# A decoder trunk in fp32: C of the state-space layer moved from the kernel's opening into the first up-projection, in two halves

## What is computed

```python
cs = silu(c)
for i in range(2):
    mod = cs @ ada_w[i] + ada_b[i]
    sh1, sc1, g1, sh2, sc2, g2 = split(mod, 6)
    h = rms_norm(x, norm1_g[i]) * (1 + sc1) + sh1
    mix = dilated_attention(h) if i == 0 else s5_mixer(h)
    x = x + g1 * mix
    h = rms_norm(x, norm2_g[i]) * (1 + sc2) + sh2
    x = x + g2 * conv_ffn(h)          # up-projection 2048 -> 2 * 5632, conv, silu(gate) * up, down
return rms_norm(x, final_norm_g)

# s5_mixer: lb = exp(a * step); coef = (lb - 1) / a; bb = coef * b
# x_t = lb * x_(t-1) + bb u_t ;  y_t = Re(c x_t) + d u_t
```

## Time and profile before

| | us |
|---|---|
| median of 3 runs | 2718.42 (2717.45 to 2720.98) |
| the profiled execution | 2721.41 |
| its span, first to last instruction | 2719.6 |
| PE busy | 2653.0 |
| VectorE busy | 2276.5 |
| ACT busy | 1293.0 |
| GpSimd busy | 512.4 |

### The profile page before, as it was taken

The page is one execution under the profiler, slowest core; times in us unless marked ns, Lnnn a source line. Parts: engine busy times, 40 slices in busy tenths (PEclk is TensorE's granted clock), DMA queues, the critical chain, the costliest instruction groups (busy, mean ns, idle before and its releaser), DMA issues.

```text
span 2719.6 us, 50038 instructions
## 1 busy us (share of the span) xinstructions
PE 2653.0 (98%) x18416; PEld 2377.3 (87%) x18416; DVE 2276.5 (84%) x3379; ACT 1293.0 (48%) x1869; POOL 512.4 (19%) x468
## 2 busy tenths in 40 slices
PE   5999999999999999999999999999999999999998
PEld 1998888888898888888888999999888888888887
DVE  6978988888889998899998988998898975677754
ACT  2444444444434655435555344444365553455543
POOL 4142201101133111000101321244411110011122
PEclk8999999999999999999999999999999999999999
DMA  9979989888876987678888968879777765655563
GB/s 377 394 254 346 339 313 344 315 318 321 317 236 219 317 285 256 203 246 307 282 284 269 375 230 250 240 250 328 256 248 250 263 182 188 200 187 190 183 191 117
DMA packets 242267, 725.47 MB, mean 267 GB/s; under 512 B 51106, under 2 KB 60066, under 8 KB 241186
## 3 DMA queue, kind: packets, MB, share of 16 engines
q1 hardware_dynamic: 185184, 666.46, 70.8%
q10 hardware_dynamic: 56900, 56.54, 6.5%
HBM read 701.66 MB, written 25.44 MB: 267 GB/s over the span
## 4 chain that ended last, share of the span: by engine, by line
PE 85%; DVE 2%; POOL 2%; issue 1%; DMA 1%; ACT 0%; ACTq 0%; POOLq 0%; DVEq 0%
PE proj L1929 28%; PE proj L1956 15%; PE proj L1936 14%; PE proj L1959 8%; PE proj L1979 5%; PE proj L1981 4%; PE proj L1980 4%; PE proj L1974 2%; PE proj L1961 1%; PE proj L1977 1%; PE ps L2102 1%; PE ps L2192 1%; DVE w_lo L1202 0%; POOL work L1785 0%; POOL work L1787 0%
## 5 line engine op out<-in xcount | busy, mean ns | idle before, releaser
L606 ACT ACTIVATE w_hi<-raw 128x1024 fp32r<-128x1024 f32 (+1 forms) x896 | 929.7, 1043 | 1118.0 <-PE proj L1936 350.8
L1202 DVE TENSOR_TENSOR w_lo<-raw,w_hi 128x1024 fp32r<-128x1024 f32 (+1 forms) x896 | 1109.9, 1244 | 352.1 <-ACT w_hi L606 341.6
L1929 PE MATMUL proj<-h_hl,w_hi 128*128 128x512 f32 x2656 | 633.7, 391 | 1.7 <-DVE x L1532 1.7
L1929 PEld LDWEIGHTS proj<-h_hl,w_hi 128*128 128x128 f32 x2656 | 488.5, 188 | 97.0 <-DVE x L1532 2.1
L1092 DVE SCALAR_TENSOR_TENSOR ada<-ada,held 128x1024 f32<-128x1024 f32 x304 | 392.5, 1291 | 0.0
L1956 PE MATMUL proj<-h_hl,w_hi 128*128 128x512 f32 x1500 | 381.0, 394 | 0.9 <-DVE work L1388 0.9
L1936 PEld LDWEIGHTS proj<-h_hl,w_lo 128*128 128x128 f32 x2656 | 340.5, 191 | 12.9
L1936 PE MATMUL proj<-h_hl,w_lo 128*128 128x256 f32 x2656 | 344.5, 283 | 0.0
L1835 POOL TENSOR_TENSOR a_hl<-work,a_hl 128x256 fp32r<-128x256 f32 (+1 forms) x88 | 119.6, 1359 | 1135.0 <-ACT a_hl L896 1135.0
L1956 PEld LDWEIGHTS proj<-h_hl,w_hi 128*128 128x128 f32 x1500 | 272.9, 189 | 51.6 <-DVE work L1388 1.2
L1979 PE MATMUL proj<-a_hl,w_hi 128*128 128x256 f32 x864 | 245.7, 284 | 0.8 <-DVE a_hl L1423 0.6
(11 more groups left out here) (287 smaller groups left out, 3369.6 us busy)
## 6 DMA issues: line engine op xcount, KB each, us to landing
raw<-in_w_up SPq DMA_DIRECT2D x352, 512.0 KB, 5.0
ada<-in_ada_t SPq DMA_DIRECT2D x304, 512.0 KB, 5.6
raw<-in_w_in SPq DMA_DIRECT2D x224, 512.0 KB, 6.4
raw<-in_w_down SPq DMA_DIRECT2D x128, 448.0 KB, 4.2
raw<-in_w_down SPq DMA_DIRECT2D x64, 512.0 KB, 3.7
ada<-in_ada_w SPq DMA_DIRECT2D x48, 512.0 KB, 9.1
raw<-in_w_out SPq DMA_DIRECT2D x32, 512.0 KB, 5.0
raw<-in_ssm_w_in SPq DMA_DIRECT2D x32, 512.0 KB, 4.9
```

What stands on the lines that cost most here:

```text
L606: nc.scalar.activation(w_hi[:, j % LAG, 0:nk * P], raw[:, j % s.ring, 0:nk * P], ACT.Copy).then_inc(hi_ready, 1)
L1202: V.tensor_tensor(w_lo[:, j % LAG, 0:nk * P], raw[:, j % s.ring, 0:nk * P], w_hi[:, j % LAG, 0:nk * P].bitcast(F32), ALU.subtract).then_in ...
L1929: mm(proj[b % 2][:, :], w_hi[:, j % LAG, (k - k0) * P:(k - k0 + 1) * P], hl[:, k].rearrange("p c t -> p (c t)"), start=(k == 0), stop=False)
```

## The change

C's load leaves the list of constants (nine instead of ten), and its buffer in the opening goes. In the first pass of the first up-projection ACT loads one half of C into `work` at step 6, at step 12 stores it once GpSimd has multiplied it and then loads the other half into the same place, and stores that at step 18. GpSimd multiplies a half in six products of 128 x 512, at its steps 0 and 14. The store in `qkv1` and the waits on it before `qkv` go; the first `load_c` waits for both stores.

GpSimd builds the table of powers first; its first part waits for the sum of squares, whose place the table takes. SP no longer waits for GpSimd's products before it loads into slot 6 of the ring.

The first eight columns of the first scale, gain * (1 + bias + sum), are made in the sums: VectorE spreads gain and gain * (1 + bias) over lanes (`gain_diag`, `bias_diag`) beforehand, PE adds the second to the running sum with four products at piece 26 of 32, and VectorE multiplies and reduces (`take_scale`) where it had multiplied, reduced, added the bias and applied the gain.

```diff
@@ build: places
-        c_raw, o = cut(a_flat, 24 * T, TILES, 2, SC)
-        lam, o = cut(a_flat, o, KT, CHUNK, 4, 2)
+        lam, o = cut(a_flat, 32 * T, KT, CHUNK, 4, 2)
-        t16a, _ = cut(raw_flat, (RAW - 1) * MODW, TILES, SC)
-        t16b, _ = cut(raw_flat, (RAW - 2) * MODW, TILES, SC)
+        c_half, o = cut(work, 0, TILES // 2, 2, SC)
+        t16a, o = cut(work, o, TILES // 2, SC)
+        t16b, o = cut(work, o, TILES // 2, SC)
+        bias_diag, o = cut(a_flat, 5 * T, MODB, 32)
+        gain_diag, _ = cut(a_flat, o, MODB, 32)
@@ SP, weights
                         sp.wait_ge(ada_summed, 2 * KT)
-                        wait(sp, prep_done, j // 6)
@@ ACT
-            act.dma_start(c_raw, a["ssm_c"]).then_inc(consts_in, 16)
...
-            act.wait_ge(consts_in, 16 * 10)
+            act.wait_ge(consts_in, 16 * 9)
...
-            def store_cw(i):
-                act.wait_ge(prep_done, 1)
-                act.dma_start(cw_d.rearrange("n p f -> p n f"), c_raw.rearrange("p (n q) a b -> p n (q a b)", q=4)
-                              ).then_inc(cw_out, 16)
...
-            late = {1: [store_lam], 8: [load_rel], 14: [store_cw], 22: [spread_lam(0)], 26: [spread_lam(1)]}
+            late = {1: [store_lam], 8: [load_rel], 22: [spread_lam(0)], 26: [spread_lam(1)]}
...
-            act.wait_ge(cw_out, 16)
...
+                            if n == 0:
+                                act.wait_ge(cw_out, 32)
...
+            def load_c_half(h):
+                def f():
+                    act.wait_ge(norm_lo, 2 * KT)
+                    wait(act, cw_out, 16 * h)
+                    act.dma_start(c_half, a["ssm_c"][:, h * TILES // 2:(h + 1) * TILES // 2]).then_inc(consts_in, 16)
+                return f
+
+            def store_c_half(h):
+                def f():
+                    act.wait_ge(prep_done, h + 1)
+                    act.dma_start(cw_d[h * KT // 2:(h + 1) * KT // 2].rearrange("n p f -> p n f"),
+                                  c_half.rearrange("p (n q) a b -> p n (q a b)", q=4)).then_inc(cw_out, 16)
+                return f
...
-                carry = {}
+                carry = {} if layer else {6: [load_c_half(0)], 12: [store_c_half(0), load_c_half(1)], 18: [store_c_half(1)]}
@@ VectorE
+            def take_scale():
+
+                dve.wait_ge(ada_summed, 2 * KT)
+                V.tensor_tensor(diag, first_ps[1], gain_diag, ALU.mult).then_inc(mod_ready, 1)
+                dve.wait_ge(mod_ready, 2)
+                V.tensor_reduce(hscale[:, 0:MODB], diag, AX.X, ALU.add).then_inc(scale_made, 1)
+                dve.wait_ge(scale_made, 2)
...
-            V.tensor_copy(hscale[:], gains[:, 0, :]).then_inc(coef_made, 1)
-            take_first(0)
+            V.tensor_scalar(hscale[:, 0:MODB], mod_b[:, 0, KT:KT + MODB], 1.0, None, ALU.add).then_inc(scale_made, 1)
+            dve.wait_ge(scale_made, 1)
+            spread = lambda v: v.unsqueeze(2).broadcast_to([P, MODB, 32])
+            V.tensor_tensor(gain_diag, lane[:].unsqueeze(1).broadcast_to([P, MODB, 32]), spread(gains[:, 0, 0:MODB]), ALU.mult
+                            ).then_inc(first_link, 1)
+            V.tensor_tensor(bias_diag, lane[:].unsqueeze(1).broadcast_to([P, MODB, 32]), spread(hscale[:, 0:MODB]), ALU.mult
+                            ).then_inc(first_link, 1)
+            take_first()
             inverse_root(0)
             low(st["qkv0"])(0, 0)
             low(st["qkv0"])(0, 1)
-            take_first(1)
-            first_scale(0)
+            take_scale()
             tiles(0, 0, 0, 0, 8)
...
-            dve.wait_ge(cw_out, 16)
@@ GpSimd
             pool.wait_ge(coef_made, 1)
-            cr, ci = c_raw[:, :, 0, :], c_raw[:, :, 1, :]
-            link(G.tensor_tensor(t16a, cr, wide(ncim, SC), ALU.mult))
-            link(G.tensor_tensor(t16b, ci, wide(cim, SC), ALU.mult))
-            link(G.tensor_tensor(cr, cr, wide(cre, SC), ALU.mult))
-            link(G.tensor_tensor(cr, cr, t16b, ALU.subtract))
-            link(G.tensor_tensor(ci, ci, wide(ncre, SC), ALU.mult))
-            G.tensor_tensor(ci, ci, t16a, ALU.add).then_inc(prep_done, 1)
             double(cos, sin)
             double(pr, pi)
+            pool.wait_ge(first_sum, 1)
...
+            def scale_c(h):
+                def f():
+                    pool.wait_ge(consts_in, 16 * (10 + h))
+                    tiles_of = slice(h * TILES // 2, (h + 1) * TILES // 2)
+                    over = lambda v: v[:, tiles_of].unsqueeze(2).broadcast_to([P, TILES // 2, SC])
+                    cr, ci = c_half[:, :, 0, :], c_half[:, :, 1, :]
+                    link(G.tensor_tensor(t16a, cr, over(ncim), ALU.mult))
+                    link(G.tensor_tensor(t16b, ci, over(cim), ALU.mult))
+                    link(G.tensor_tensor(cr, cr, over(cre), ALU.mult))
+                    link(G.tensor_tensor(cr, cr, t16b, ALU.subtract))
+                    link(G.tensor_tensor(ci, ci, over(ncre), ALU.mult))
+                    G.tensor_tensor(ci, ci, t16a, ALU.add).then_inc(prep_done, 1)
+                return f
...
-                carry = {}
+                carry = {} if layer else {0: [scale_c(0)], 14: [scale_c(1)]}
@@ TensorE
+                if n == 26:
+                    pe.wait_ge(first_link, 2)
+                    for g in range(4):
+                        rows = slice(32 * g, 32 * g + 32)
+                        mm(first_ps[1][rows], ident[:, rows], bias_diag, start=False, stop=False)
```

More of the change, by code:

```diff
@@ L1156, in tiles, with take_first, second_scale @@
                 tile_low(number, mod_layer, shift, k0 + nk - 1)
[L1158 to L1163, removed]
+            def take_first():
+                cols = slice(0, MODB)
+                dve.wait_ge(ada_summed, KT)
+                V.tensor_tensor(diag, first_ps[0], lane[:].unsqueeze(1).broadcast_to([P, MODB, 32]), ALU.mult
                                 ).then_inc(first_link, 1)
-                dve.wait_ge(first_link, 2 * q + 1)
+                dve.wait_ge(first_link, 3)
                 V.tensor_reduce(mod[:, 0, cols], diag, AX.X, ALU.add).then_inc(first_link, 1)
-                dve.wait_ge(first_link, 2 * q + 2)
+                dve.wait_ge(first_link, 4)
                 V.tensor_tensor(mod[:, 0, cols], mod[:, 0, cols], mod_b[:, 0, cols], ALU.add).then_inc(mod_ready, 1)
-            def first_scale(half):
-                ks = slice(half * KT // 2, (half + 1) * KT // 2)
-                dve.wait_ge(mod_ready, 2 * half + 2)
+            def take_scale():
[4 more added lines that the diff above has]
+                dve.wait_ge(scale_made, 2)
+            def second_scale():
+                ks = slice(KT // 2, KT)
+                dve.wait_ge(mod_ready, 4)
                 V.scalar_tensor_tensor(out=hscale[:, ks], in0=mod[:, 0, KT:2 * KT][:, ks], scalar=1.0,
                                        in1=gains[:, 0, ks], op0=ALU.add, op1=ALU.mult).then_inc(scale_made, 1)
-                dve.wait_ge(scale_made, half + 1)
+                dve.wait_ge(scale_made, 3)
             def take_fifth(i):
@@ L1205, in f @@
                         k = s.old[j]
-                        if k == 0:
-                            dve.wait_ge(prep_done, 1)
                         dve.wait_ge(ada_in[k % ADA], 16 * (5 + k // ADA + 1))
@@ L1313, in _ @@
             V.tensor_tensor(lam[:, :, 0, :, 1], four(m3), four(m4), ALU.add).then_inc(lam_made, 1)
-            for _ in range(2):
-                link(V.tensor_tensor(mag[:], mag[:], mag[:], ALU.mult))
+            link(V.tensor_tensor(mag[:], mag[:], mag[:], ALU.mult))
+            V.tensor_tensor(mag[:], mag[:], mag[:], ALU.mult).then_inc(coef_made, 1)
             dve.wait_ge(first_sq, KT)
@@ L1319, in _ @@
             dve.wait_ge(first_sum, 1)
-            dve.wait_ge(consts_in, 16 * 10)
-            V.tensor_copy(hscale[:], gains[:, 0, :]).then_inc(coef_made, 1)
-            take_first(0)
+            dve.wait_ge(consts_in, 16 * 9)
+            V.tensor_scalar(hscale[:, 0:MODB], mod_b[:, 0, KT:KT + MODB], 1.0, None, ALU.add).then_inc(scale_made, 1)
[6 more added lines that the diff above has]
+            take_first()
             inverse_root(0)
@@ L1339, in second_half @@
                 take_early(1)
-                first_scale(1)
+                second_scale()
                 dve.wait_ge(norm_lo, 8)
@@ L1357, in norm @@
                 low(st[following])(0, LO_FIRST - 1)
-                dve.wait_ge(scale_made, number + 2)
+                dve.wait_ge(scale_made, number + 3)
                 tiles(number, mod_layer, shift, 0, KT)
@@ L2059, in _ @@
                 if n == 18:
-                    pe.wait_ge(consts_in, 16 * 10)
+                    pe.wait_ge(consts_in, 16 * 9)
                     pe.wait_ge(lam_made, 1)
```

## The result

The changed kernel takes 2734.78 us in the median of 6 runs (2731.98 to 2740.10), the kernel before 2719.38 (2717.45 to 2720.98, also 6). The ratio is 1.0056, 95% interval 1.0046 to 1.0067: slower by 0.56%, and above the predicted range. The profiled execution took 2731.98 us around a span of 2730.2, so the two traces differ by only 10.6 us: the one of after comes from the fastest of its six runs, that of before from a run above its median.

The account below looks back on a forecast made before the run. The prediction took bytes to bound the opening and PE the rest. From 2721.4 us, -2.6 in the opening and +7.4 in the up-projection gave 2726.2; lowered 3.0 to the median of runs, 2723.2, range 2713.5 to 2730.

Parts of the forecast that it names:

- the two costs in the up-projection: First up-projection: GpSimd's products delay VectorE, and ACT waits for half 0's store; together +7.4 us.
- GpSimd beside VectorE: First up-projection: each product makes VectorE 0.58 us late, six products 3.5 us; bounds for a half 1.2 and 6.2.
- the rival of the full lock: First up-projection: each product holds VectorE for its whole 1.04 us, costing +12.8, total 2728.6 us; chance 0.13.
- The store's landing: First up-projection, step 12: ACT waits 5.0 us until half 0's store has landed; bounds 2.2 and 10.9.
- the clock in the opening: Opening, 80 to 130 us, in a rival with chance 0.13: granted clock 0.97 in the mean, 1.5 us lost.
- the prediction's own steps: First up-projection: split at 899.4, store landed 905.4, addition 906.6, PE 4.4 us late; half 1 adds 3.0.
- The opening: Without C's load, transfers behind it come sooner by its bytes: -2.6 us; bounds 0 and -6.3.
- PE's first product: Opening, a sign: PE's first product comes at about 60.3 us instead of 63.26.
- The late weight: End of the opening, about 128 us: comes 2.6 us sooner; no sooner or much more than 3 refutes the prediction.
- The first scale: Opening: made in the sums, it gains PE's path 0.4 us, but the weights at 129 us decide: 0.
- the table first: Opening: VectorE's first tiles and sums run without GpSimd beside them, but the late weight hides the relief: 0.
- the store that left the second pass: Second pass over the query weights: C's store goes, but PE is the bound there: 0.

Follow-up runs that it names:

- the opening alone: The changed kernel without the loads, products and stores of C in the first up-projection; 2718.16 us.
- neither: The changed kernel with a place of its own for C's second half and without GpSimd's products: the halves are only loaded and stored; 2715.84 us.
- the second pass: The changed kernel with C loaded, multiplied and stored in the second pass over the query weights, not in the up-projection; 2717.74 us.
- The load alone: The kernel before without the load of C in the opening, its place filled with ones by GpSimd; 2717.55 us.
- the second trace of before: The kernel before, unchanged, run once more for a second trace of its opening; 2720.74 us.
- half-size products: The changed kernel with a place for each half of C and 24 GpSimd products of 128x256 instead of 12 of 128x512; 2725.78 us.
- other steps: The changed kernel, one place, with ACT storing half 0 at step 10, loading half 1 at 14 and storing it at 21; 2727.01 us.
- two places: The changed kernel with a place of its own for the second half of C, so its load no longer waits for the first store; 2725.48 us.
- products on VectorE: The changed kernel with a place for each half of C and the twelve products made by VectorE, one in each of steps 8 to 19; 2723.57 us.

## Why the prediction was wrong

**The direction and the two costs in the up-projection were right, their sizes were not, and a third cost was left out.** Forecast were 2723.2 us and at most 2730, measured are 2734.78. Predicted were +7.4 us in the up-projection; it is +16.5 in the traces and 16.6 to 18.9 between the medians of the changed kernel and the three with the same opening (2715.84 to 2718.16).

*GpSimd beside VectorE: taken 0.58 us a product, measured 0.88.* The 0.58 of the earlier trace rows is the mean of 0.79, 0.51 and 0.44, and only in the first did a step meet nearly a whole product (0.92 us of 1.04). Timelines of the kernel before, GpSimd and VectorE:

```profile
181.44 1.37 POOL L1774 TENSOR_TENSOR before<-before,zero 128x512 f32<-128x512 f32 x1
182.89 1.90 POOL L1775 TENSOR_TENSOR before<-before,zero 128x512 f32<-128x512 f32 x1
```

```profile
181.83 0.41 DVE L1379 TENSOR_TENSOR work<-proj,work 128x256 f32<-128x256 f32 x1
...
183.82 0.41 DVE L1379 TENSOR_TENSOR work<-proj,work 128x256 f32<-128x256 f32 x1
```

Before the second and the third residue step an addition that reads PSUM ran inside the product, unstretched, so that the step behind it met only the rest of that product: it started 0.64 us before the end of the one and 0.57 before the end of the other. In the up-projection six steps with both inputs in SBUF follow one another, and each meets nearly a whole product. 0.88 lies above the 0.65 from which the rival of the full lock was to decide, so that rival had this term better; its 2728.6 was still 6.2 us short, for the two terms below. The Trainium skill, "SBUF — State Buffer", section "SBUF: two separate sides", says that the lock concerns VectorE instructions in a two-port mode or with two SBUF inputs. The trace agrees on the second: the addition with one input in PSUM keeps its 0.41.

*The store's landing: taken 5.0 us, measured 9.0, and 10.8 without the products.* Half the bytes of the whole store needed nearly the whole store's 10.9 us of the earlier trace rows; half 1 took 8.0 in both kernels. The argument that fewer weights are asked for while the engines stand still did not hold: the DMA share stays at 0.89 and 1.04 from the store's issue to its landing (first two rows below).

*The clock: not in the sum.* Windows of the changed kernel around its longest wait:

```profile
895.00:901.00 6.00, 5.83 (x32) 4.98 (x32) 4.67 (x7) 1.85 (x3) 0.00 (x0) 1.00 0.89 276
901.00:905.40 4.40, 0.00 (x0) 0.00 (x0) 0.39 (x1) 0.80 (x2) 0.00 (x0) 0.87 1.04 395
905.40:909.00 3.60, 3.51 (x8) 2.81 (x9) 3.08 (x5) 3.48 (x6) 2.52 (x2) 0.50 0.38 146
909.00:912.00 3.00, 3.00 (x11) 2.37 (x10) 2.96 (x3) 0.00 (x0) 2.84 (x3) 0.66 0.69 197
```

PE idles 4.7 us; then the granted clock is 0.50, which is 1.2 GHz, up to 909 us and 0.66 in the mean up to 912, and the block's high products take 2.7 us longer. The prediction charged the clock in the opening and forgot it where it made PE wait.

Put into the prediction's own steps, 5.3 and 9.0 give: split at 901.2, landing at 911.2, addition at 912.4, 10.2 us late, and 4.8 from half 1: 15.0, against 14.8 by the block starts. Of the 7.6 us that this adds to 7.4, 4.0 are the landing and 1.8 GpSimd in each half. The sum agrees better than its parts, which is luck: the store went out before the split and not behind it, which took some 1.8 us off, half 1 cost 3.8 and not 4.8, and the clock put 2.7 on.

**The opening: the cause was right; the medians agree with the term, the traces show about twice as much.** Taken -2.6, by the bytes of C. Nine traces with the changed opening have norm 1 at 855.7 to 858.7, 856.9 in the mean, the two of before at 862.0: 5.1 sooner. The medians of the three kernels with this opening and no loss behind it (the opening alone, neither, the second pass) say 1.7 to 3.8, 2.6 in the mean. The load alone brings 4.4 in its trace. Window of the changed kernel, against the second of the earlier trace rows:

```profile
50.00:80.00 30.00, 23.19 (x161) 19.22 (x154) 24.57 (x34) 12.24 (x19) 4.17 (x8) 0.77 1.02 402
```

402 GB/s for 388 over 30 us is 1.0 us of bytes more than the term counted. PE's first product came at 59.12 where 60.3 was named. The late weight of the earlier trace rows was to come 2.6 us sooner, and much more than 3 was named as a sign of being wrong. Timeline of ACT after, the split of the same weight and the next one:

```profile
122.82 1.06 ACT L606 ACTIVATE w_hi<-raw 128x1024 fp32r<-128x1024 f32 x1 [1.23 <-DMA raw<-in_w_in]
...
124.89 1.06 ACT L606 ACTIVATE w_hi<-raw 128x1024 fp32r<-128x1024 f32 x1 [0.73 <-PE proj L2007]
```

The split stood at 128.35 before, so the weight came 5.5 us sooner (5.3 against the second trace of before, 128.08): the sign was met. After it ACT waits for PE, and no late weight decides any more. What brings the part beyond 3.6 us of bytes was not isolated. How much of the 5.1 is real for the time is not settled: 2.6 lies within all three intervals, and so does no gain, in one at its edge; 5.1 lies within one. The traced runs may exaggerate it, since the two of before lie 2.0 and 2.2 us above their medians and the nine others 0.6 below theirs in the mean.

**What was costed at nothing.** The first scale, the table first and the store that left the second pass: the opening of before without load and products has norm 1 at 857.79, among the nine traces of the changed one. The extra bytes in the up-projection: nothing, by the kernel that only loads and stores.

## What to carry to other kernels

Work for an idle engine is not free when its instructions hold up those of the busiest one: price it in that engine's time, here 0.88 us for an instruction of 1.07, and put it where that engine has time in hand (71 of 90 us busy, and not 54 of 56). A wait for a DMA in an engine's queue costs the whole landing of the transfer for everything behind it; a few steps between issue and wait saved nearly as much as a second buffer. Where a new wait makes TensorE idle, reckon with a slower block behind it: here it added 1.6 to 2.7 us, or nothing.

## What was not expected of the hardware

The length of a wait did not decide whether the granted clock fell. Behind waits of 2.05 (half-size products), 2.43 (other steps), 2.66 and 2.79 us (two places) the next block's high products took 5.5 us instead of 3.8, but behind 2.15 (products on VectorE), 2.78 and 3.62 us (the changed kernel) they took 3.92 to 3.94. The wait in the next up-projection shown with the opening alone is 1.74 to 1.79 us long in all fourteen traces; the block behind it took 5.5 us in five of them and 3.9 in nine. Such differences of 1.6 to 1.7 us may be part of the changed kernel's spread of 8 us over six runs; that was not tried.

ACT issued the store of step 12 at 895.08, ahead of the activation at 895.49 and the split at 895.80, which both stand before it in its program: so a DMA issue did not wait here for the activations ahead of it, while the copy behind a waiting issue did wait, 7.75 us.
